# Order of the products in the MLPs of a two-layer trunk: both column halves per group, or one half after the other

## The chip, the cores and the metric

The kernel runs on one core of a Trainium2 chip. The metric is the time on the device in microseconds (us); lower is better. The engines named below are TensorE (PE; its weight loads have a track of their own, PEld), VectorE (DVE), ScalarE (ACT), GpSimd (POOL) and SyncE (SP), whose queue issues the DMAs here.

## The reference, cut to what matters

The program is one inference step of a trunk with two layers, for 512 latent tokens and 128 context tokens (640 columns in all) of width 1024. Layer 0 mixes with attention and a gated linear recurrence, layer 1 with a bidirectional RWKV-7 recurrence. After each mixer comes an MLP with 4096 hidden units, which is where the change is:

```python
def sq_relu_mlp(h, w1, w2):
    return jnp.square(jax.nn.relu(h @ w1)) @ w2

for l in range(DEPTH):                      # DEPTH = 2
    ...                                     # mixer
    h = modulate(rms_norm(x, W['norm2_w'][l]), sh2, sc2)
    x = x + gt2 * sq_relu_mlp(h, W['mlp_w1'][l], W['mlp_w2'][l])
```

## The kernel before, in words

Everything is laid out with channels on the partitions and the 640 tokens in the free dimension. The stages run one after the other; each engine meets the others at the end of each (`stage_end`). Instructions on an engine run in program order, and the order is written out by hand with semaphores.

**The stage of an MLP** has three parts that overlap. First the norm: for each of eight channel groups k, ACT squares (L420) and PE sums over channels; then ACT makes the reciprocal root (L423, L424); then, group by group, DVE scales (L450), ACT shifts (L433) into a buffer, and DVE splits the result into two float32r tensors, `norm_high` by a cast (L490) and `norm_low` by a subtraction (L492). Each finished group increments `norm_split`. The products of the MLP use these pairs: high times high, low times high, high times low, so three products stand for one of full precision.

Second the weights. They come in 32 blocks of 1 MB a layer: two halves of the hidden units, each with eight "up" blocks (256 hidden units, from all 8 groups of channels) and eight "down" blocks (128 output channels, from 16 groups of hidden units). SP loads a block (L505), ACT casts it to `weights_high` (L545), DVE subtracts to get `weights_low` (L549).

Third the products, in `mlp_pe` (L508 to L529). A tile is 128 outputs by 640 columns; it takes a pair of PSUM banks, 320 columns in each, and tiles alternate between two pairs. An up block has two tiles, a down block one. For a tile the loops are: group k (`kt`, 8 for up, 16 for down), then the term (three of them), then the column half g2. So each group issues six matmuls of 128x320, which write the first and the second bank in turn. All matmuls of the helper `mm` are recorded at L169. A layer has 32 up tiles of 48 matmuls and 16 down tiles of 96, 3072 matmuls in all.

The very first tile waits before each group for `norm_split` of that group, so it runs along with the norm's split. The first down tile of each half waits before each group for `hidden_split` of that group. The tile's last matmul increments `mlp_product`, once for both halves. After it, for an up tile, ACT applies the relu to both banks at once (L570), DVE squares (L583) and splits into `hidden_high` and `hidden_low` (L490, L492); for a down tile DVE adds the gated result to x (L590). PE waits for the evacuation of the tile before the previous one.

After the second MLP the result is turned by PE (L2008), copied by ACT (L2015) and stored. Other stages use ordinary fp32 matmuls in two forms that matter below. In `products`, a "cm" tile writes 512 columns in one bank and 128 in the next for each group; a "tm" tile writes 512 columns (the variant "tmk" 128) in one bank only, for all its groups. Each fp32 product is two matmul instructions in the trace.

Of the kernel before, what the change touches and what calls it, by code (L numbers as in the profile page):

```python
# [22 lines left out]
KT = D // P  # L23
# [76 lines left out]
HIDT = DFF // 2 // P  # L100
# [12 lines left out]
def program(nc, a, o):  # L113
    with ExitStack() as ctx:
# [22 lines left out]
        def S(name):  # L137
            if name not in sems:
                sems[name] = ctx.enter_context(nc.semaphore(name))
            return sems[name]  # L140
# [26 lines left out]
        def mm(out, lhsT, rhs, start=True, stop=True, shared=False):  # L167

            return nc.tensor.matmul(out, lhsT, rhs, start=start, stop=stop, skip_group_check=shared)  # L169
# [39 lines left out]
        for l in range(LAYERS):  # L209
            if l == 0:  # L210
                ada_stage(0)
                w = a["ab_w_in"][0]
# [53 lines left out]
        b = 0  # L266
# [241 lines left out]
        def mlp_pe(pe, l):  # L508
            for n, (half, kind, b) in enumerate(BLOCKS):
                g, kt = NBLK * l + n, (KT if kind == "up" else HIDT)  # L510
                pe.wait_ge(S("mlp_weights_low"), g + 1)
                first = n == 0
                wh, wl = (x.rearrange("p (k n) -> p k n", k=kt) for x in (WHI[:, g % 2, :], WLO[:, g % 2, :]))
                xh, xl = (NH, NL) if kind == "up" else (HH, HL)
                for j in range(tiles_before[n + 1] - tiles_before[n]):
                    t = tiles_before[n] + j
                    if t >= 2:
                        wait_evacuated(pe, l, t - 2)
                    pb, c = 2 * (t % 2), slice(128 * j, 128 * j + 128)
                    for k in range(kt):  # L520
                        if kind == "down" and b == 0:
                            pe.wait_ge(S("hidden_split"), 2 * HIDT * l + HIDT * half + k + 1)
                        if first and j == 0:
                            pe.wait_ge(S("norm_split"), KT * l + k + 1)
                        for term, (w, x) in enumerate(((wh, xh), (wh, xl), (wl, xh))):
                            for g2 in range(2):
                                ins = mm(PS[:, pb + g2, 0:HN], w[:, k, c], x[:, k, HN * g2:HN * g2 + HN],
                                         start=k == 0 and term == 0, stop=k == kt - 1 and term == 2)
                    ins.then_inc(S("mlp_product"), 1)  # L529

        def wait_evacuated(pe, l, t):

            n = max(i for i in range(NBLK) if tiles_before[i] <= t)
            half, kind, b = BLOCKS[n]
            if kind == "up":
                pe.wait_ge(S("up_evacuated"), 2 * HIDT * l + HIDT * half + 2 * b + t - tiles_before[n] + 1)
            else:
                pe.wait_ge(S("down_evacuated"), 16 * l + 8 * half + b + 1)
# [1524 lines left out]
        def _(pe):  # L2063
# [15 lines left out]
            stage_end(pe, "pe")  # L2079
            norm_pe(pe, 1)  # L2080
            mlp_pe(pe, 0)
            stage_end(pe, "pe")
            norm_pe(pe, 2)
# [6 lines left out]
            stage_end(pe, "pe")  # L2090
            norm_pe(pe, 3)
            mlp_pe(pe, 1)
            stage_end(pe, "pe")
            out_pe(pe)
# [114 lines left out]
```

## Time and profile before

| | us |
|---|---|
| median of 3 runs | 2601.51 |
| lowest and highest | 2600.41, 2604.34 |
| the profiled execution, own time | 2601.19 |
| its span | 2599.4 |
| PE busy | 2299.6 (88%) |
| DVE busy | 1049.8 (40%) |
| ACT busy | 821.6 (32%) |

The span runs from the first instruction to the last, and the profiled execution took 1.8 us more than it. PE's busy time counts matmuls whose ends are modelled and that overlap, so the distance between the starts of two matmuls says more than the mean duration. "PEclk" is the granted clock of PE, 1.00 for full (2.4 GHz) and 0.50 for half (1.2 GHz).

### The profile page before, as it was taken

The page shows a single profiled execution, that of the slowest core. Times are in us where ns is not written, and L with a number is a line of the kernel's source. Part 1 is how long each engine was busy: PE and PEld are TensorE (multiplying, and loading weights), DVE is VectorE, ACT ScalarE, POOL GpSimd, SP SyncE. Part 2 cuts the span into 40 slices and gives each one's busy share as a digit, 9 for nine tenths or more (in the row PEclk, how much of TensorE's full clock was granted, in tenths as well). Part 3 has the DMA queues.
Part 4 walks back from the last instruction along what each step waited for, and adds up shares of the span by engine and source line. Part 5 has one row for each costly group of instructions (what it writes and reads, how often), then busy time and mean ns, then how long its engine had stood idle before and what let it go on. Part 6 is the DMA issues. An engine that isn't in the chain of part 4 may idle for free. (4 is left out here: it accounts for less than half of the span.)

```text
span 2599.4 us, 57953 instructions
## 1 busy us (share of the span) xinstructions
PE 2299.6 (88%) x25851; PEld 1814.5 (70%) x25851; DVE 1049.8 (40%) x2099; ACT 821.6 (32%) x1660; POOL 289.3 (11%) x526
## 2 busy tenths in 40 slices
PE   5999967678899999989998688888888789999999
PEld 2555435354599999975543567666667459999998
DVE  0000056551443244224114777777775134423421
ACT  3211145440321122121001676666664032111211
POOL 0000013210000000000000343444433000000000
PEclk8999979788999999999999899999999789999999
DMA  8223100751122222210110000000000202322221
GB/s 301 104 91 129 43 3 1 263 199 34 33 81 66 81 76 71 81 65 33 65 41 21 7 7 9 9 9 9 9 6 5 98 16 82 81 66 81 74 74 57
DMA packets 160740, 167.70 MB, mean 65 GB/s; under 512 B 13788, under 2 KB 117996, under 8 KB 160364
## 3 DMA queue, kind: packets, MB, share of 16 engines
q1 hardware_dynamic: 160492, 164.00, 19.5%
q8 instruction: 204, 3.34, 0.5%
q14 instruction: 44, 0.36, 0.0%
HBM read 160.44 MB, written 3.54 MB: 63 GB/s over the span
## 5 line engine op out<-in xcount | busy, mean ns | idle before, releaser
L169 PE MATMUL psum<-arena 64*64 64x64 f32 (+7 forms) x17920 | 1139.9, 267 | 197.0 <-ACT arena L1591 30.9
L169 PEld LDWEIGHTS psum<-arena 64*64 64x64 f32 (+3 forms) x17920 | 768.5, 150 | 569.6 <-issue 386.0
L169 PE MATMUL psum<-norm_high,weights_high 128*128 128x320 f32 x1024 | 237.6, 314 | 16.2 <-DVE norm_low L492 16.1
L169 PE MATMUL psum<-norm_low,weights_high 128*128 128x320 f32 x1024 | 235.6, 312 | 0.0
L169 PE MATMUL psum<-norm_high,weights_low 128*128 128x320 f32 x1024 | 235.3, 311 | 0.0
L169 PE MATMUL psum<-hidden_low,weights_high 128*128 128x320 f32 x1024 | 233.4, 309 | 0.0
L169 PE MATMUL psum<-hidden_high,weights_low 128*128 128x320 f32 x1024 | 233.4, 309 | 0.0
L169 PE MATMUL psum<-hidden_high,weights_high 128*128 128x320 f32 x1024 | 233.3, 309 | 0.0
L545 ACT ACTIVATE weights_high<-weights 128x2048 fp32r<-128x2048 f32 x62 | 118.5, 1911 | 338.4 <-PE psum L169 338.4
L169 PEld LDWEIGHTS psum<-norm_high,weights_high 128*128 128x128 f32 x1024 | 172.6, 190 | 20.5 <-issue 10.8
L169 PEld LDWEIGHTS psum<-norm_low,weights_high 128*128 128x128 f32 x1024 | 173.4, 190 | 0.0
L169 PEld LDWEIGHTS psum<-norm_high,weights_low 128*128 128x128 f32 x1024 | 173.4, 190 | 0.0
L169 PEld LDWEIGHTS psum<-hidden_high,weights_high 128*128 128x128 f32 x1024 | 171.4, 188 | 0.0
L169 PEld LDWEIGHTS psum<-hidden_high,weights_low 128*128 128x128 f32 x1024 | 171.4, 188 | 0.0
L169 PEld LDWEIGHTS psum<-hidden_low,weights_high 128*128 128x128 f32 x1024 | 171.2, 188 | 0.0
L590 DVE SCALAR_TENSOR_TENSOR arena<-psum,ada,arena 128x320 f32<-128x320 f32 (+2 forms) x96 | 36.3, 434 | 314.6 <-PE psum L169 314.6
L549 DVE TENSOR_TENSOR weights_low<-weights,weights_high 128x2048 fp32r<-128x2048 f32 x64 | 146.4, 2288 | 26.8 <-ACT weights_high L545 26.7
L570 ACT ACTIVATE relu<-psum 128x640 f32<-128x640 f32 x64 | 45.0, 703 | 342.5 <-PE psum L169 342.5
L583 DVE TENSOR_TENSOR relu<-relu 128x640 f32<-128x640 f32 x64 | 52.8, 825 | 234.3 <-ACT relu L570 234.3
L169 PE MATMUL psum<-arena,constants 64*64 64x128 f32 (+3 forms) x430 | 111.3, 496 | 39.5 <-ACT arena L420 13.5
L618 ACT ACTIVATE arena<-psum 128x640 f32<-128x640 f32 x40 | 28.1, 703 | 319.9 <-PE psum L169 319.9
L169 PEld LDWEIGHTS psum<-arena,constants 64*64 64x64 f32 (+1 forms) x430 | 50.1, 175 | 98.7 <-issue 67.6
(178 smaller groups left out, 2104.5 us busy)
## 6 DMA issues: line engine op xcount, KB each, us to landing
weights<-in_mlp_w SPq DMA_DIRECT2D x64, 1024.0 KB, 5.7
arena<-in_ada_w SPq DMA_DIRECT2D x24, 2048.0 KB, 9.6
arena<-in_ab_w_in SPq DMA_DIRECT2D x6, 2048.0 KB, 8.2
arena<-in_ab_w_out SPq DMA_DIRECT2D x2, 2048.0 KB, 8.9
arena<-in_rwkv_wr SPq DMA_DIRECT2D x2, 2048.0 KB, 10.4
arena<-in_rwkv_wk SPq DMA_DIRECT2D x2, 2048.0 KB, 8.3
arena<-in_rwkv_wv SPq DMA_DIRECT2D x2, 2048.0 KB, 8.1
arena<-in_rwkv_wo SPq DMA_DIRECT2D x2, 2048.0 KB, 11.2
```

What stands on the lines that cost most here:

```text
L169: return nc.tensor.matmul(out, lhsT, rhs, start=start, stop=stop, skip_group_check=shared)
L545: A.activation(WHI[:, g % 2, :], WRAW[:, g % 2, :], ACT.Copy).then_inc(S("mlp_weights_high"), 1)
L549: V.tensor_tensor(WLO[:, g % 2, :], WRAW[:, g % 2, :], WHI[:, g % 2, :], ALU.subtract)\
L570: A.activation(TMP[:, u % 2, :].rearrange("p (g n) -> p g n", g=2), PS[:, 2 * (t % 2):2 * (t % 2) + 2, 0:HN], ACT.Relu).then_inc(S("up_eva ...
L583: step(V.tensor_tensor(x, x, x, ALU.mult))
L590: ins = V.scalar_tensor_tensor(x, PS[:, 2 * (t % 2) + t0 // HN, c:c + t1 - t0], ADAS[:, l, 40 + b, g:g + 1], x, ALU.mult, ALU.add)
L618: ins = A.activation(unit(x), pair(pb), func(x))
```

## The change

In `mlp_pe` the loop over the column half g2 moves from the innermost place to the outermost within a tile. Matmuls, operands, banks and start and stop flags of each bank are the same; their order within a tile isn't. The two waits stand inside the loop over k and so are issued twice in a tile that has them.

```diff
-                    for k in range(kt):
-                        if kind == "down" and b == 0:
-                            pe.wait_ge(S("hidden_split"), 2 * HIDT * l + HIDT * half + k + 1)
-                        if first and j == 0:
-                            pe.wait_ge(S("norm_split"), KT * l + k + 1)
-                        for term, (w, x) in enumerate(((wh, xh), (wh, xl), (wl, xh))):
-                            for g2 in range(2):
+                    for g2 in range(2):
+                        for k in range(kt):
+                            if kind == "down" and b == 0:
+                                pe.wait_ge(S("hidden_split"), 2 * HIDT * l + HIDT * half + k + 1)
+                            if first and j == 0:
+                                pe.wait_ge(S("norm_split"), KT * l + k + 1)
+                            for term, (w, x) in enumerate(((wh, xh), (wh, xl), (wl, xh))):
                                 ins = mm(PS[:, pb + g2, 0:HN], w[:, k, c], x[:, k, HN * g2:HN * g2 + HN],
                                          start=k == 0 and term == 0, stop=k == kt - 1 and term == 2)
                     ins.then_inc(S("mlp_product"), 1)
```

## Rows read from the trace of the kernel before

**Rows 1.** The chain of waits, layer 1's MLP: start us, us, what.
```profile
2137.90 0.83 DVE norm_low L492
2138.73 0.74 DVE arena L450
2139.46 0.41 DVE norm_high L490
2139.88 0.02 issue
2139.90 0.83 DVE norm_low L492
2140.74 0.04 issue
2140.78 447.10 PE psum L169 x3036
2587.88 0.02 issue
2587.90 0.55 DVE arena L590
```

**Rows 2.** Busy time by windows: busy us (count) for each engine, PEclk, DMA share, GB/s.
```profile
core 0: us, PE busy (x) PEld busy (x) DVE busy (x) ACT busy (x) POOL busy (x), PEclk, DMA share, GB/s
800.00:900.00 100.00, 100.00 (x684) 100.00 (x683) 29.28 (x33) 14.71 (x9) 0.00 (x0) 1.00 0.27 74
2330.00:2430.00 100.00, 100.00 (x684) 100.00 (x683) 38.40 (x43) 19.30 (x16) 0.00 (x0) 1.00 0.24 74
```

**Rows 3.** Timeline amid an up tile: start, us, engine, line, op, tiles, count [idle <-releaser].
```profile
760.72 0.33 PEld L169 LDWEIGHTS psum<-norm_high,weights_high 128*128 128x128 f32 x2
760.86 0.46 PE L169 MATMUL psum<-norm_high,weights_high 128*128 128x320 f32 x2
761.01 0.34 PEld L169 LDWEIGHTS psum<-norm_low,weights_high 128*128 128x128 f32 x2
761.15 0.46 PE L169 MATMUL psum<-norm_low,weights_high 128*128 128x320 f32 x2
761.30 0.34 PEld L169 LDWEIGHTS psum<-norm_high,weights_low 128*128 128x128 f32 x2
761.45 0.46 PE L169 MATMUL psum<-norm_high,weights_low 128*128 128x320 f32 x2
```

**Rows 4.** Timeline of layer 0's first tile: group 0, then groups 5 to 7.
```profile
691.18 0.87 PE L169 MATMUL psum<-norm_high,weights_high 128*128 128x320 f32 x2 [5.22 <-DVE norm_low L492]
691.85 0.74 PE L169 MATMUL psum<-norm_low,weights_high 128*128 128x320 f32 x2
692.39 0.73 PE L169 MATMUL psum<-norm_high,weights_low 128*128 128x320 f32 x2
...
701.09 0.57 PE L169 MATMUL psum<-norm_high,weights_high 128*128 128x320 f32 x2 [0.84 <-DVE norm_low L492]
...
703.09 0.57 PE L169 MATMUL psum<-norm_high,weights_high 128*128 128x320 f32 x2 [0.84 <-DVE norm_low L492]
...
703.56 0.83 DVE L492 TENSOR_TENSOR norm_low<-norm_whole,norm_high 128x640 fp32r<-128x640 f32 x1
...
704.44 0.56 PE L169 MATMUL psum<-norm_high,weights_high 128*128 128x320 f32 x2 [0.20 <-DVE norm_low L492]
```

**Rows 5.** Busy time by windows, first tile of layer 0, then of layer 1.
```profile
691.00:693.00 2.00, 1.82 (x6) 1.57 (x6) 1.97 (x5) 1.19 (x2) 0.00 (x0) 0.50 0.00 0
697.00:699.00 2.00, 1.20 (x7) 0.88 (x6) 1.97 (x5) 1.20 (x3) 0.00 (x0) 1.00 0.02 4
703.00:705.00 2.00, 1.72 (x10) 1.46 (x11) 1.52 (x4) 1.80 (x1) 0.00 (x0) 1.00 0.00 0
...
2132.00:2134.00 2.00, 1.97 (x7) 1.57 (x7) 1.97 (x4) 1.20 (x3) 0.00 (x0) 0.50 0.00 0
2134.00:2136.00 2.00, 1.61 (x9) 1.09 (x8) 1.97 (x4) 1.20 (x3) 0.00 (x0) 1.00 0.00 0
2138.00:2140.00 2.00, 1.15 (x6) 0.89 (x6) 1.97 (x4) 1.20 (x3) 0.00 (x0) 1.00 0.00 0
2140.00:2142.00 2.00, 1.22 (x5) 1.22 (x5) 1.96 (x3) 2.00 (x3) 0.00 (x0) 0.71 0.00 0
2142.00:2144.00 2.00, 2.00 (x9) 2.00 (x9) 1.55 (x2) 0.50 (x1) 0.00 (x0) 0.50 0.00 0
2144.00:2146.00 2.00, 2.00 (x15) 2.00 (x14) 1.69 (x3) 0.70 (x1) 0.00 (x0) 0.94 0.03 10
```

**Rows 6.** Timeline of layer 1's first tile, its last groups.
```profile
2141.26 0.83 DVE L492 TENSOR_TENSOR norm_low<-norm_whole,norm_high 128x640 fp32r<-128x640 f32 x1
...
2142.53 0.74 PE L169 MATMUL psum<-norm_high,weights_high 128*128 128x320 f32 x2
```

**Rows 7.** Timeline where the first down tile begins.
```profile
811.02 0.46 PE L169 MATMUL psum<-hidden_high,weights_high 128*128 128x320 f32 x2
811.22 0.70 ACT L570 ACTIVATE relu<-psum 128x640 f32<-128x640 f32 x1 [6.34 <-PE psum L169]
...
813.35 0.83 DVE L492 TENSOR_TENSOR hidden_low<-relu,hidden_high 128x640 fp32r<-128x640 f32 x1
```

**Rows 8.** Timeline of PE in the fp32 input projection (cm, tmk and tm tiles).
```profile
103.94 17.85 PE L169 MATMUL psum<-arena 128*128 128x512 f32 x112
121.72 1.92 PE L169 MATMUL psum<-arena,silu_c_rows 128*32 128x512 f32 x16
123.58 1.05 PE L169 MATMUL psum<-constants,arena 128*128 128x2 f32 x8
124.49 34.86 PE L169 MATMUL psum<-arena 128*128 128x512 f32 x128
159.28 1.92 PE L169 MATMUL psum<-arena,silu_c_rows 128*32 128x512 f32 x16
...
237.16 34.58 PE L169 MATMUL psum<-arena 128*128 128x512 f32 x80
271.67 1.92 PE L169 MATMUL psum<-arena,silu_c_rows 128*32 128x512 f32 x16
```

## The prediction
> **What bounds the kernel now.** I read the chain of waits first. It ends in layer 1's MLP: a relay between DVE and ACT makes the split norm, one group about every 2 us, until the group that is ready at 2140.74, and from there PE runs 3036 matmuls in 447.10 us without one wait [rows 1]. The windows say the same of both layers: 684 matmuls start in 100 us, PEclk 1.00, while DVE has 29 to 38 us of work and ACT under 20 [rows 2]. So an MLP is a tile's worth of waiting for the norm, then a bare stream of matmuls. A change of order can act in three places: the distance between two matmuls of the stream, the first tile (which waits for the norm group by group), and the first down tile (which waits for the hidden groups).
>
> **The stream, per matmul.** 100 us / 684 is 146.2 ns; the chain gives 447.10 / 3036 = 147.3 ns, which includes some slow matmuls (below). Within a tile pairs start at 760.86, 761.15 and 761.45 [rows 3]: 0.293 us a pair, 0.1467 us a matmul. I use 0.1467. 320 columns at 2.4 GHz take 133.3 ns, so 13.4 ns of each matmul are something else. The pairs share their weights, and the distance in a pair (durations: two matmuls end 0.46 after the start, one lasts 0.31, so the second starts 0.15 later) is that between pairs. So neither new weights nor new moving data costs more than the same ones. What the trace of the MLPs can't show is the bank, since there every matmul switches banks. After the change only each 24th (up) or 48th (down) does.
>
> The nearest rows for the bank are fp32. Four cm tiles switch banks on every second matmul: 128 matmuls from 124.49 to 159.28, 34.79 us; their columns (two passes of 512, or of 128, at 2.4 GHz, mean 266.7 ns) are 34.13 us, so 5.1 ns a matmul is extra. Five tm tiles never switch within a tile: 80 matmuls from 237.16 to 271.67, 34.51 us; their columns are 34.13 us, 4.7 ns extra [rows 8]. One switch for two matmuls thus costs at most 0.8 ns per switch. By that a gain of the change is at most 0.8 x 6144 = 4.9 us. For a loss (same bank again and again) the narrow tmk tiles are the worst row: 112 matmuls from 103.94 to 121.72 take 17.78 us; 32 of them are one cm tile (8.70 at the rate above), which leaves 9.08 us for 80, 113.5 ns each against 106.7 of columns; 6.8 is 1.7 ns more than the cm rate. As a loss that is at most 1.7 x 6144 = 10.4 us. I take 0: the widest same-bank row (tm) is nearer in columns, and it lies within 0.4 ns.
>
> [...]
>
> **The first tile of each MLP.** Before, all six matmuls of group k follow as soon as its split is there, so after the last group (7) only 6 of the tile's 48 are left. Changed, the pass over the first half issues 3 per group at the norm's pace, and after the last split come 3 for the first half and then all 24 of the second, since PE runs in order and can't start the second half while it waits in the first. DVE's and ACT's pace doesn't depend on PE here, so the last split comes when it did. The tile is 27 matmuls from its end at that point, not 6: 21 x 0.1467 = 3.1 us later, in each layer. Nothing covers it: the stream behind it has no waits to absorb a delay [rows 1, 2].
>
> Layer 0: the last split ends at 704.39 and PE, waiting, starts group 7 at 704.44 [rows 4]. Cost 3.1 us.
>
> Layer 1: here the clock had fallen (PEclk 0.71, then 0.50) just before the end of the norm [rows 5], PE was late, and took up group 7 at 2142.53 though its split ended at 2142.09 [rows 6]. With half of the work ahead of it, PE will be waiting. 0.4 us come back.
>
> **The clock in the first tile.** At half clock a matmul takes 0.267 us (0.54 a pair: 691.85, 692.39 [rows 4]). Before, PE enters each first tile at 0.50, is busy for 1.57 us of each 2 with its weight loads, or 1.97 with modelled ends, and the clock goes to 1.00 about 6 us after the first product, at 697 and 2134 [rows 5]. With three matmuls a group at that clock, 0.8 of each 2 us is work. The rows with so little work are the later groups, six warm matmuls in 2 us (0.88 us): in layer 0 the clock stayed up with them until the dense part came, in layer 1 it fell at about 2141. No row shows it rise from half with so little. I take it that it stays down through the norm, and that the dense part after the last split starts at half clock. How long it stays there: layer 1 shows dense work from 2140.78 and the clock back by 2144.2 (0.71, 0.50, 0.94 over three windows are 3.4 us at half), 3.4 us; the first tiles show up to 6. I take 4.5 us. Each us at half clock loses 1 - 0.1467/0.267 = 0.45 us, so 2.0 us a layer. Layer 1 paid for 1.7 us of this already (2142.53 to about 2144.2), 0.8 us, which goes.
>
> [...]
>
> **The first down tile of each half.** The tile's first matmul is at 811.02, the hidden group it needs last is split at 813.35 + 0.83 = 814.18 [rows 7]. Before, PE came to it after 90 matmuls (824.2); now after 45 x 0.1467 = 6.6 us, at 817.6. 3.4 us of cover are left: cost 0. Without it, each us late would count four times over, two halves in two layers. The 80 waits issued a second time in the program find their semaphores already raised, and the tile with 16 waits runs at the distance of all others: 0.
>
> **Evacuation and loads.** The increment still comes at the tile's end for both banks, ACT and DVE read the pair while PE is in the other pair, and weight blocks are freed at block ends: 0, everything shifts with PE.
>
> **Sum.** Layer 0: 3.1 + 2.0 = 5.1. Layer 1: 3.1 - 0.4 + 2.0 - 0.8 = 3.9. Together +9.0 us, all on the path. The profiled execution took 2601.19 us in all, so 2610.2; the median of the runs is 0.3 above that execution, so 2610.5. With the clock at its best +5.0, with 6.8 us at half clock in each layer +11.1. With the bounds of the bank term the likeliest case's own range is 2602 to 2623.
>
> **Rivals.**
> *The clock rises anyway* during the first tile's sparse pass, or with the first dense matmul. Then only 3.1 + 1.9 = 5.0 us are added: 2606.5, at the border of what can be told. For it: before, it rose in this place in both layers [rows 5]. Against: with twice the work.
> *Banks.* The 13.4 ns beyond the columns are, wholly or in part, the switch of bank with every matmul, which only the MLPs have. Place: every matmul of both streams. Price: each ns less is 6.1 us; from 1.5 ns on the sum of +9.0 is paid, and beyond 2.3 ns it is faster by more than can be called noise. Wholly so: 6144 x 13.4 = -82, about 2528. For it: the excess is there only in the alternating stream (fp32 has 4.7 to 6.8). Against: fp32 cm tiles switch for 0.8 ns at most [rows 8], and at half clock the distance is 0.267, the bare columns, where a fixed cost per switch would still show.
> *Same bank costs.* Adding to a bank just written delays each matmul by more than the tmk rows' bound; at 3 ns +18 us beside the +9: 2629. For it: the tmk rows' small excess. Against: tm rows.
> *Nothing happens*: the waits per group turn out to be hidden. The chain excludes it, unless gains of the bank by up to 0.8 ns cancel it: 2601.5 + 9.0 - 4.9 = 2605.6.
>
> **How the numbers follow.** A measurement of this kernel tells 0.2%, 5.2 us, from no change. Likeliest case 0.62 (all slower, save at the edge of its low end), clock rises 0.13 (half slower, half same), small gain of the bank 0.07 (same), banks 0.09 (faster), same bank costs 0.09 (slower). Faster 0.09, same 0.16, slower 0.75. The range 2603 to 2619 leaves out "banks" and the greater part of "same bank costs", and takes in the rest.
>
> **What would show it.** In each first tile: groups of three matmuls 2 us apart with PE idle longer between them; after the last split 27 matmuls to the relu of tile 0, and PEclk 0.50 there for some us. In the stream: still 684 matmuls in 100 us. At 811 and the like: no wait of PE. The prediction is wrong if the windows amid a layer count more or fewer than 682 to 686 matmuls, or if the first tile ends less than 3 us after where it ended.

## The result and the profile after

| | before | changed |
|---|---|---|
| median of 9 runs, us | 2600.41 | 2611.02 |
| lowest and highest | 2594.23, 2604.34 | 2606.42, 2615.69 |
| profiled execution, its span | 2601.19, 2599.4 | 2610.77, 2609.0 |
| PE busy | 2299.6 | 2304.7 |

The ratio is 1.0042, 95% interval 1.0029 to 1.0054: slower, by 10.6 us by the medians (7.5 to 14 by the interval). The forecast was 2610.5. (The three runs of before that the forecast started from had a median of 2601.51.)

The chain of waits in the changed kernel, layer 1 (start us, us, what), answers to [rows 1]:

```profile
2147.80 0.83 DVE norm_low L492
2148.63 0.04 issue
2148.68 448.76 PE psum L169 x3051
2597.44 0.02 issue
2597.46 0.55 DVE arena L590
```

The chain now follows DVE to the very last split (group 7; groups are counted from 0), and 3051 matmuls are left there. Before, it left DVE one group earlier with 3036 to go, of which 6 were group 6's, so 3030 were left from the last split on. 3051 - 3030 = 21, as counted. The windows of the changed kernel (busy us and count by engine, PEclk, DMA share, GB/s), against [rows 2, 5]:

```profile
697.00:699.00 2.00, 1.17 (x4) 0.77 (x4) 1.97 (x4) 1.20 (x2) 0.00 (x0) 0.50 0.00 0
701.00:703.00 2.00, 1.81 (x6) 1.41 (x7) 1.52 (x3) 1.59 (x1) 0.00 (x0) 0.50 0.00 0
703.00:705.00 2.00, 2.00 (x9) 2.00 (x9) 1.92 (x1) 0.00 (x0) 0.00 (x0) 0.50 0.00 0
705.00:707.00 2.00, 2.00 (x10) 2.00 (x9) 0.00 (x0) 0.00 (x0) 0.00 (x0) 0.50 0.38 86
707.00:709.00 2.00, 2.00 (x15) 2.00 (x15) 0.00 (x0) 0.33 (x1) 0.00 (x0) 0.98 1.06 372
800.00:900.00 100.00, 100.00 (x684) 100.00 (x683) 29.11 (x34) 16.50 (x11) 0.00 (x0) 1.00 0.27 74
...
2148.00:2150.00 2.00, 1.82 (x7) 1.42 (x7) 1.55 (x2) 1.04 (x1) 0.00 (x0) 0.50 0.00 0
2150.00:2152.00 2.00, 2.00 (x13) 2.00 (x12) 1.36 (x1) 0.00 (x0) 0.00 (x0) 0.77 0.00 0
2152.00:2154.00 2.00, 2.00 (x15) 2.00 (x15) 0.00 (x0) 0.06 (x1) 0.00 (x0) 1.00 0.66 173
2330.00:2430.00 100.00, 100.00 (x684) 100.00 (x683) 36.03 (x41) 19.52 (x16) 0.00 (x0) 1.00 0.24 74
```

Two things are to be seen. Amid a layer 684 matmuls start in 100 us, to the unit as before, so the bank makes no difference. And the clock, which before was full from 697 on in layer 0 and from 2134 on in layer 1, with one fall [rows 5], now stays at half through the norm and for some us of dense work behind it. The timeline of the changed kernel shows groups 6 and 7 of layer 0, against [rows 4]:

```profile
700.88 0.64 PE L169 MATMUL psum<-norm_high,weights_high 128*128 128x320 f32 x1 [0.83 <-DVE norm_low L492]
701.31 0.47 PE L169 MATMUL psum<-norm_low,weights_high 128*128 128x320 f32 x1
701.35 0.83 DVE L492 TENSOR_TENSOR norm_low<-norm_whole,norm_high 128x640 fp32r<-128x640 f32 x1
701.58 0.47 PE L169 MATMUL psum<-norm_high,weights_low 128*128 128x320 f32 x1
702.23 0.64 PE L169 MATMUL psum<-norm_high,weights_high 128*128 128x320 f32 x1 [0.19 <-DVE norm_low L492]
```

There are three matmuls per group and then the wait; after 702.23 matmuls follow without one. Tile 0's relu, which marks the end of the first tile, starts at 708.67, 6.5 us after the last split; before it started 1.2 us after it:

```profile
705.62 0.70 ACT L570 ACTIVATE relu<-psum 128x640 f32<-128x640 f32 x1 [0.82 <-PE psum L169]
```

So the tile ends 5.3 us later in layer 0, and in layer 1 3.0 us later (5.3 against 2.3 after the last split). At the first down tile the first matmul is at 814.07 and the split it needs last (below) ends at 817.22. PE comes to that group 45 matmuls of 0.1467 us later, at 820.7, and doesn't wait:

```profile
816.40 0.82 DVE L492 TENSOR_TENSOR hidden_low<-relu,hidden_high 128x640 fp32r<-128x640 f32 x1
...
820.67 0.31 PE L169 MATMUL psum<-hidden_high,weights_high 128*128 128x320 f32 x1
```

The timelines give, for each MLP, the time from the first start of a product to the last (us), and the time from the end of the last norm split to the last product's start:

```
                        first to last product    last split to last product
                        layer 0    layer 1       layer 0    layer 1
before                  457.61     458.68        444.41     445.47
changed                 462.88     461.70        449.67     448.49
```

So layer 0 got 5.3 us longer and layer 1 3.0, 8.3 in all. The spans differ by 9.6. The rest is elsewhere: what precedes the first MLP was 2.2 us shorter in this profile, what lies between the MLPs 3.5 longer (983.6 against 980.1).

### The profile page after: what moved, and what is told of

It is laid out like the page before. It is cut to its first block and busy times, and to the rows that moved or that the text cites. A ratio compares the mean times of both kernels' runs of the same rounds, so it can differ in the third digit from the quotient of the medians.

```text
span 2609.0 us, 57953 instructions
## 1 busy us (share of the span) xinstructions
PE 2304.7 (88%) x25851; PEld 1818.0 (70%) x25851; DVE 1049.9 (40%) x2099; ACT 822.0 (32%) x1660; POOL 290.2 (11%) x526
## 5 line engine op out<-in xcount | busy, mean ns | idle before, releaser
L169 PE MATMUL psum<-norm_high,weights_high 128*128 128x320 f32 x1024 | 322.7, 315 | 20.7 <-DVE norm_low L492 20.7
L169 PE MATMUL psum<-norm_low,weights_high 128*128 128x320 f32 x1024 | 320.0, 313 | 0.0
L169 PE MATMUL psum<-norm_high,weights_low 128*128 128x320 f32 x1024 | 319.8, 312 | 0.0
L169 PE MATMUL psum<-hidden_high,weights_high 128*128 128x320 f32 x1024 | 316.4, 309 | 0.0
L169 PE MATMUL psum<-hidden_low,weights_high 128*128 128x320 f32 x1024 | 316.4, 309 | 0.0
L169 PE MATMUL psum<-hidden_high,weights_low 128*128 128x320 f32 x1024 | 316.4, 309 | 0.0
L169 PEld LDWEIGHTS psum<-norm_high,weights_high 128*128 128x128 f32 x1024 | 194.9, 190 | 26.6 <-DVE norm_low L492 15.8
L169 PEld LDWEIGHTS psum<-norm_low,weights_high 128*128 128x128 f32 x1024 | 195.6, 191 | 0.0
L169 PEld LDWEIGHTS psum<-norm_high,weights_low 128*128 128x128 f32 x1024 | 195.5, 191 | 0.0
L169 PEld LDWEIGHTS psum<-hidden_low,weights_high 128*128 128x128 f32 x1024 | 192.2, 188 | 0.0
L169 PE MATMUL psum<-arena,constants 64*64 64x128 f32 (+3 forms) x430 | 111.1, 497 | 39.5 <-ACT arena L420 13.5
```

## Experiments

Each time is beside runs of the kernel before on the same chip.

**Where the cost sits: the first tile alone, and all tiles but the first.** In both, the loops of a tile are written as a list of (half, group, term), and one line picks the tiles (the rest of the edit is left out here):

```diff
+                    halves_outside = first and j == 0          # first_tile_only
+                    halves_outside = not (first and j == 0)    # all_but_first
```

> Only the first tile of each MLP has the halves outside the groups; all others as before. First-tile theory: all of the cost is here, so +8 to +10 us against before, and the time from the first product to the last is 462 to 463 us in layer 0 and about 462 in layer 1, as with the whole change. Rival (the cost is spread over the stream, a ns or two a matmul): within 2 us of before.

Measured: 2610.08 against 2600.14, ratio 1.0042 (1.0027 to 1.0057), +9.9 us. First to last product 461.94 and 461.88 us. One changed tile a layer gives the whole cost, as the first-tile theory has it.

> All tiles but the first of each MLP have the halves outside. First-tile theory: no change, within 2 us of before, and products last 457.6 us in layer 0 and 458.7 in layer 1 as before. Rival (spread over the stream): +8 to +10 us. Rival (banks: fewer switches save, the first tile costs more than it seems): several us faster than before.

Measured: 2599.85 against 2600.14, ratio 0.9998 (0.9989 to 1.0006). First to last product 457.61 and 457.62. The chain of this kernel in layer 1, then its window in layer 0:

```profile
2140.80 0.04 issue
2140.85 444.68 PE psum L169 x3030
2585.52 0.02 issue
```
```profile
800.00:900.00 100.00, 100.00 (x684) 100.00 (x683) 27.63 (x32) 14.72 (x9) 0.00 (x0) 1.00 0.27 75
```

94 of the 96 tiles have the new order here, and nothing moved. Both theories that lay the cost, or a gain, in the stream are out. The run shows one more thing: with the order of before in the first tile, layer 1 can be as fast as layer 0 (457.62). The 458.68 of the kernel before was the clock that happened to fall at 2141 in that profile [rows 5], not a property of the order.

> The changed kernel itself, on the same chip as its three variants: +8 to +10 us against before by every theory; it is the measure for the others.

Measured: 2611.81, ratio 1.0046 (1.0033 to 1.0059), +11.7 us; first to last product 461.94 and 462.92.

**Order and clock taken apart.** The first pass of the first tile gets filler, which are matmuls of no use, written into a bank that nobody reads:

```diff
                                          start=k == 0 and term == 0, stop=k == kt - 1 and term == 2)
+                            if first and j == 0 and g2 == 0 and k < KT - 1:
+                                for _ in range(6):
+                                    mm(PS[:, 6, 0:HN], wh[:, k, c], xh[:, k, 0:HN])
```

> The whole change, with six further matmuls of no use (into a bank that nobody reads) behind each group's three in the first pass of the first tile, all groups but the last. They fill PE's waits, so the clock should be full when the last split comes. Theory (order 21 matmuls late plus the clock): the clock's part goes, +5 us against before instead of +8 to +10 (layer 0 +3.1, layer 1 +1.9). Rival (the clock costs nothing, all is order): stays at +9.

Measured: 2606.56 against 2600.14, ratio 1.0030 (1.0019 to 1.0041), +6.4 us. Its windows over the end of the norm in layer 0, and its chain in layer 1:

```profile
699.00:701.00 2.00, 1.59 (x11) 1.32 (x11) 1.96 (x4) 1.55 (x3) 0.00 (x0) 1.00 0.00 0
701.00:703.00 2.00, 2.00 (x15) 1.97 (x15) 1.51 (x3) 1.45 (x1) 0.00 (x0) 1.00 0.00 0
703.00:705.00 2.00, 2.00 (x16) 2.00 (x15) 1.77 (x1) 0.00 (x0) 0.00 (x0) 1.00 0.00 0
```

```profile
2144.28 0.04 issue
2144.33 449.12 PE psum L169 x3060
```

The chain leaves DVE one group before the last, with that group's three matmuls, six of filler and 3051 others to go. The clock is full, and from the last split to the last product it takes 447.49 us in both layers, 3.08 more than the 444.41 of an undisturbed layer in the order of before (one whose clock doesn't fall again): 21 x 0.1467 = 3.08. That is the order's term to the hundredth. What the other kernels with the late order have beyond 447.49 is the clock's: 2.18 and 1.00 (changed), 1.25 and 1.19 (first_tile_only), 1.24 and 2.22 (changed_again). The two kernels with the late order that are told of below had 2.17 and 1.30, and 2.17 and 1.27. By the times alone +6.4 (4.9 to 10.7) doesn't exclude the rival's +9; the profile does. My +5 had counted 1.2 us that the kernel before loses in layer 1 only when its clock falls.

**The theory turned round: both first tiles at once.** If what counts is how many matmuls are left at the last split, the second tile of the first block needn't stand behind the norm either (`...` marks what is cut from a line):

```diff
+                if first:
+                    for k in range(KT):
+                        pe.wait_ge(S("norm_split"), KT * l + k + 1)
+                        for j in range(2):
+                            c = slice(128 * j, 128 * j + 128)
+                            for term, (w, x) in enumerate(((wh, xh), (wh, xl), (wl, xh))):
+                                for g2 in range(2):
+                                    ins = mm(PS[:, 2 * j + g2, 0:HN], ...)
+                            if k == KT - 1:
+                                ins.then_inc(S("mlp_product"), 1)
+                    continue
```

> The kernel before, but the first block's two tiles are made together: for each group as it comes, six matmuls for tile 0 (banks 0, 1) and six for tile 1 (banks 2, 3). First-tile theory (what counts is how many matmuls are left when the last split comes): tile 1 no longer stands behind the norm. Dense from the first product, so the clock rises after 3 to 6 us; the block ends about 16.4 us after the first product (96 x 0.1467, and 2.3 lost at half clock) instead of 21.2: -4.8 us a layer, -8 to -11 us against before. Rival (the norm's relay or the weights' split of block 1, ready 15.95 us after the first product, sets the end anyway): -2 us or less.

Measured: 2593.37 against 2601.49, ratio 0.9968 (0.9958 to 0.9977), -8.1 us. First to last product 452.73 and 453.10: 4.9 and 4.5 below an undisturbed 457.6. Its chain in layer 1, and its windows at the start of layer 0's products:

```profile
2124.97 16.69 PE psum L169 x96
2141.67 0.01 issue
2141.67 436.73 PE psum L169 x2976
```
```profile
689.00:691.00 2.00, 2.00 (x8) 2.00 (x9) 1.97 (x4) 1.20 (x2) 0.00 (x0) 0.50 0.00 0
691.00:693.00 2.00, 2.00 (x9) 2.00 (x9) 1.97 (x4) 1.20 (x2) 0.00 (x0) 0.50 0.00 0
693.00:695.00 2.00, 2.00 (x15) 2.00 (x14) 1.97 (x4) 1.20 (x2) 0.00 (x0) 0.94 0.00 0
```

PE is dense from the first product, and the 96 matmuls, 14.1 us at the full clock, end the block after 16.69; the clock was at half for the first 4.5 us of them in layer 0 and 5.3 in layer 1.

Next, filler in the norm keeps the clock up ahead of the first product:

> As two_tiles_at_once, and in each norm ahead of an MLP five fp32 matmuls of 512 columns of no use, while PE waits for the reciprocal root. With the clock full at the first product the block is bound by the last split plus 12 matmuls, 15.0 us after the first product, and then by block 1's weights at 16.0: -5.2 us a layer, 0.5 to 1 us better in all than two_tiles_at_once. Rival (clock of no account): the same as two_tiles_at_once.

```diff
                 mm(PS[:, 1, 0:NP_], ...).then_inc(S("norm_sum"), 1)
+            if i % 2:
+                for _ in range(5):
+                    mm(PS[:, 6, 0:NS], con(C_MEAN), sq[:, 0:NS])
```

Measured: 2590.90 against 2601.49, ratio 0.9963 (0.9952 to 0.9974), -10.6 us. First to last product 452.44 twice, together 0.95 less than in two_tiles_at_once; the 2.5 us between the two medians are more than that, but their intervals overlap. The clock is full throughout the first tiles, and a new wait is what remains; the chain of this kernel in layer 1:

```profile
2137.89 2.30 DVE weights_low L564
2140.19 0.04 issue
2140.23 436.75 PE psum L169 x2976
```

Block 1's split weights come last now, as expected. Next, DVE splits them ahead of the norm (the edit also takes block 1 out of the two later loops that split weights, which is left out here):

```diff
             mlp_low(dve, g, 0, l)
+            g += 1
+            dve.wait_ge(S(f"mlp_loaded{g % 2}"), 16 * (g // 2 + 1))
+            V.tensor_copy(WHI[:, g % 2, :], WRAW[:, g % 2, :]).then_inc(S("mlp_weights_high"), 1)
+            mlp_low(dve, g, 1, l)
```

> As two_tiles_warm, and DVE casts and subtracts block 1's weights too before the norm, in its idle time, so that nothing of block 1 is late. First-tile theory: -6.2 us a layer (42 matmuls x 0.1467), -11 to -13.5 us against before, the best of all. Rival (the relay gets longer by the work moved ahead of it): the first product comes later and the gain is that of two_tiles_warm or less.

Measured: 2591.85 against 2601.49, ratio 0.9967 (0.9954 to 0.9979), -9.6 us; first to last product 452.10 twice, 5.5 below 457.6 and not 6.2. Against two_tiles_warm, which it was to beat, the products are 0.34 us a layer shorter and the time isn't (2591.85 against 2590.90, within the spread). The third tile waits for tile 0's relu, which tile 0, ending six matmuls before tile 1, gives too late:

```profile
704.76 0.70 ACT L589 ACTIVATE relu<-psum 128x640 f32<-128x640 f32 x1 [3.02 <-PE psum L169]
705.15 0.46 PE L169 MATMUL psum<-norm_high,weights_low 128*128 128x320 f32 x2
705.61 0.53 PE L169 MATMUL psum<-norm_high,weights_high 128*128 128x320 f32 x2
```

The pair at 705.61 is the third tile's first and starts 0.46 us behind the pair before it instead of 0.29. Four banks of their own for the first two tiles remove that (the relu then reads these banks too, left out here):

```diff
-                                    ins = mm(PS[:, 2 * j + g2, 0:HN], ...)
+                                    ins = mm(PS[:, 4 + 2 * j + g2, 0:HN], ...)
-                    if t >= 2:
+                    if t >= 4:
                         wait_evacuated(pe, l, t - 2)
```

> As two_tiles_warm_early, but the first block's two tiles use banks 4 to 7, so the third tile, in banks 0 and 1, doesn't wait for tile 0's relu. The 0.75 us between last split and end that two_tiles_warm_early had beyond its 2988 matmuls (438.89 against 438.15) should go in each layer: 438.15 in both, -1.5 us in all against two_tiles_warm_early, -11 to -13 against before. Rival (the gap is the weights of block 1 or 2): 438.9 stays.

Measured: 2589.01 against 2602.47, ratio 0.9954 (0.9936 to 0.9972), -13.5 us. First to last product 451.87 and 451.86. From the last split 438.67 and 438.65 are left: 0.2 of the 0.75 went, the size of the wait for the relu, and not all. The chain has no wait left in it:

```profile
2122.16 0.84 DVE norm_low L495
2123.00 0.14 issue
2123.14 452.18 PE psum L169 x3072
2575.32 0.02 issue
```

The rest of the 0.75 was the last two splits, which come 1.35 us apart: the 12 matmuls of group 6 take 1.76, and their first two start 0.1 us late each (701.32 and 701.57 in this trace), so that PE takes up group 7 at 703.18, over 0.5 us behind the end of its split at 702.62. I had put all of it down to the bank.

**What lies between the MLPs.** In the changed kernel the sums of the norm after the first MLP ran at half clock at first, in the kernel before at full; the sums in the timeline (changed, then before):

```profile
1155.57 11.61 PE L169 MATMUL psum<-arena,constants 128*128 128x512 f32 x32 [3.42 <-ACT arena L420]
```
```profile
1152.52 8.92 PE L169 MATMUL psum<-arena,constants 128*128 128x512 f32 x32 [3.42 <-ACT arena L420]
```

The windows of the two stretches show the clock (changed, then before):

```profile
1155.00:1157.00 2.00, 1.43 (x2) 0.84 (x3) 0.00 (x0) 1.05 (x2) 0.00 (x0) 0.50 0.97 361
```
```profile
1152.00:1154.00 2.00, 1.48 (x5) 0.90 (x6) 0.00 (x0) 1.13 (x3) 0.00 (x0) 1.00 0.95 346
```

The sums took 2.7 us longer, of the 3.5 by which this stretch was longer. Filler was put ahead of them, four fp32 products and then two:

```diff
+            if i == 2:
+                for _ in range(4):          # 2 in changed_two_fill
+                    mm(PS[:, 6, 0:NS], con(C_MEAN), unit(U_X)[:, 0:NS])
```

> The whole change, and at the start of the norm that follows the first MLP four fp32 matmuls of no use while PE waits for the squares. In four profiles with the late order that norm's sums took 10.5 us at half clock at first, in two with the order of before 8.9. Theory (a part of the change's cost beyond the two first tiles is the clock in this norm): -1.6 us against the changed kernel, so +7 to +9 against before. Rival (chance of single profiles): as the changed kernel, +9 to +11.5.

Measured: 2611.92 against 2601.49, ratio 1.0042 (1.0027 to 1.0057), +10.4. There is no gain in the time, and it was a poor test: the filler took 3.4 us, more than the 2.1 of the wait that it could fill, and held the sums up itself.

> As changed_busy_next_norm, with two fp32 matmuls of no use instead of four: four ran until 1158.8, past the first square (1157.3), so PE was late with the sums whatever the clock; two end before it. Theory (clock in this norm): its sums take 8.9 us instead of 10.5 to 11, -1.6 us in the profile's stage against the changed kernel. Rival (two are too few for the clock to stay): 10.5 us again. By its time alone the two are hard to tell apart (+7.5 to +10 against before).

Measured: 2610.41 against 2602.47, ratio 1.0029 (1.0019 to 1.0039), +7.9. The timeline has filler and sums in one piece of 36 matmuls; it starts earlier by the filler, and its clock is full (window behind it):

```profile
1151.88 11.00 PE L169 MATMUL psum<-arena,constants 128*128 128x512 f32 x36 [1.27 <-DVEq L163]
```
```profile
1153.00:1155.00 2.00, 1.93 (x6) 0.63 (x5) 0.00 (x0) 1.50 (x3) 0.00 (x0) 1.00 0.91 257
```

The sums end 12.6 us after the last product's start, as in the kernel before (12.65), instead of 14.3 to 15.3 in the three late kernels without filler. So the clock was full where the filler stood; in the times the intervals of this kernel and the changed one overlap. That it was the filler which kept the clock up isn't shown by this profile alone: two of the ten profiles without filler there had it full as well, and so had all three with it.

> As two_tiles_own_banks, and the two fp32 matmuls of changed_two_fill at the start of the norm after the first MLP. If that fill keeps the clock up, another -1.6 us, -12 to -15 against before and the best of all; if not, as two_tiles_own_banks.

Measured: 2588.84 against 2602.47, ratio 0.9954 (0.9941 to 0.9966), -13.6 us: as two_tiles_own_banks, within what can be told. The profile has the sums' end 12.6 us after the last product's start, against 14.3 in two_tiles_own_banks, but the 1.6 us that were expected of it don't show in the medians (2588.84 and 2589.01). With either, the kernel is 0.45% faster than before and 0.9% faster than the changed one by these ratios.

## Why the prediction was right

The direction, the place and the mechanism held, and the time came out within 0.5 us (2610.5 forecast, 2611.02 measured). That closeness is luck: the forecast was 2601.5 + 9.0, the runs gave 2600.4 + 10.6, and the two errors nearly cancel.

- **The stream, 0 us**: right. There were 684 matmuls in 100 us, and all_but_first took the time of before. The 0.8 ns a switch that the fp32 rows allowed [rows 8] is not there either, and "banks" and "same bank costs" are out. What the 13.4 ns beyond the columns are stays open. A change of bank is excluded as their cause, and so is a change of weights or of the moving operand [rows 3]; the weight load that stands before every matmul in all these kernels (683 beside 684 in each window) isn't, since none of them left it out.
- **21 matmuls late, 3.1 us a layer**: right. It measured 3.08 in both layers with the clock kept full.
- **The clock stays at half, 2.0 us a layer**: right in kind, somewhat too large. It was 1.0 to 2.2 us in six layers of three profiles, mean 1.5, and 1.3 to 2.2 in the four layers of changed_busy_next_norm and changed_two_fill. I took 4.5 us of dense work at half clock; it was 4.9 (702.2 to about 707) and 2.3 (2148.6 to about 2151).
- **Layer 1 gives back 1.2 us** (0.4 and 0.8): right for that profile as arithmetic (3.0 us between the two profiles where 3.9 was forecast, the rest being the clock's size), wrong as a property of the kernel. Layer 1 of all_but_first, with the old order in its first tile, had no such loss. In the three other first tiles with that order the clock stayed up, so I should have charged it at its chance.
- **The down tiles, 0**: right. 3.4 us of cover were forecast; 817.22 against 820.7 are 3.5.
- **The sum**: 9.0 forecast; the MLPs measured 8.3 between the two profiles, 9.6 between the spans. Against an undisturbed old order it is 2 x (3.08 + 1.5) = 9.2. The medians say 10.6, and their interval (7.5 to 14) holds all of these. Whether the 1 to 2 us that remain are caused by the change isn't settled: the norm after the first MLP was slow in the three kernels with the late order and in first_tile_kept_busy, and fast in the two with the old one; but it was slow as well (14.3 to 15.6 us to the end of the sums) in all four kernels with two tiles at once and no filler there, which aren't late. In profiles alone a lucky clock can't be told from a cause.

## What to carry to other kernels

In a stage that consumes a producer's pieces as they come, count the consumer's instructions that are left when the last piece arrives: where nothing behind them waits, they are the cost. An order is good if it does all that can be done with each piece before it waits for the next (here -8.1 us by two tiles at once, and -13.5 with the clock, the weights and the banks seen to as well). Moving a loop outward over such a wait costs the instructions that it puts behind it (21 here) once, however long the stream that follows. An engine that has less to do during the wait may also stay at the lower clock, and pay for that behind the wait; filler in its idle time tells the two apart.

## What the runs showed of the hardware

At the full clock a float32r matmul of 128x320 starts every 146.7 ns, whether each one changes the PSUM bank (before) or 47 in a row go on in the bank of the one ahead (changed). At half clock one starts every 267 ns, which is its 320 columns alone.

With three such matmuls every 2 us the clock was at half for the whole norm in each of ten first tiles (five kernels). With six every 2 us it became full 4.7 to 5.8 us after the first product in four first tiles (before and all_but_first), and in one of these four it then fell again, at 2140.8 in before; with nine every 2 us, filler among them, it became full after 4.5 and 4.7 us. With five fp32 products of filler in the idle time before the first product it was full throughout, in eight first tiles of four kernels.
